# Row sums of the last norm carried through the additions in memory, and three of its tiles shared out to ScalarE and GpSimd

## The chip, the core and the metric

The kernel runs on one core of a Trainium2 chip. The metric is the device time of one execution in microseconds. The core's engines are TensorE (PE; its weight loads are PEld), VectorE (DVE), ScalarE (ACT), GpSimd (POOL) and SyncE (SP), which only issues transfers here. On-chip memory is SBUF (128 partitions) and PSUM (8 banks of 512 float32 columns in each partition), into which TensorE writes.

## The reference

One layer of a hybrid decoder for 1024 prompt rows and 8 sample rows of width 1024. A mixer of four branches comes first, then a first norm, a mixture of 16 SwiGLU experts of which each row uses two, and a last norm:

```
x <- LN(ALPHA * x + Mixer(x));  x <- LN(ALPHA * x + MoE(x))

def layer_norm(x, g, b):
    xf = x.astype(jnp.float32)
    mu = xf.mean(-1, keepdims=True)
    var = jnp.square(xf - mu).mean(-1, keepdims=True)
    return ((xf - mu) * lax.rsqrt(var + LN_EPS) * g + b).astype(x.dtype)

    out = jnp.zeros(xt.shape, jnp.float32)
    for e in range(N_EXPERTS):
        h = jax.nn.silu(xt @ w1_l[e]) * (xt @ w3_l[e])
        out = out + gate[:, e:e + 1] * (h @ w2_l[e])
```

## The kernel before, in words

The 1032 rows are nine tiles of 128 (the sample tile, number 0 in the order used here, has 8 rows). Every large product is made of three products of parts: an operand is split into a rounded part and its remainder, ScalarE making the first (`w13_high`, `w2_high`, `rows_high`), VectorE the second (`w13_low`, `w2_low`, `rows_low`).

After the mixer each tile gets its first norm (`normed`, the row x1 in `acc`), the router picks two experts for each row, and the rows are scattered by GpSimd's indirect transfers into a buffer in memory ordered by expert (`xs`, rows of `DX` columns: the 1024 of x1, then two gate columns, the group's top expert and the row's number). SP also writes x1 itself to a buffer in memory, `yd` (`store_x1`).

Then 32 work items follow, each up to 128 rows of one expert (16 experts, 16 possible overflows). In item q TensorE makes the hidden product of item q+1 in two halves (`hidden`), transposes the rows of item q+2, then the down product of item q (`down`) in two halves of 512 columns. ScalarE takes each half out of PSUM, times the row's gate, into one of four buffers `yo` (`out_low`, L1002 and L1004), and GpSimd adds the buffer into the rows of `yd` by an accumulating indirect transfer (`add_rows`, L1593). Items that can share rows wait for each other's additions. `yd` thus ends as x1 plus the experts' sum (divided by ALPHA, which the norm takes out).

The end: SP loads the last norm's weights `ln2` (L567, L568), waits for all additions, loads the nine tiles of `yd` back into `acc` (L574) and stores each finished tile (L579). For each tile ScalarE makes a pass for the row sum (L1054), scales it to minus the mean (L1056), makes a pass for the sum of squares (L1058) and a square root (L1060); VectorE's `finish` takes the reciprocal (L1565) and makes two products over the tile (L1567: plus minus-mean, times the weight; L1568: times the reciprocal, plus the bias). The tiles go in the order 0 to 8 on every engine, each engine working through its own list, with semaphores between them (`yg` a tile is loaded, `sd` its square root is there, `y_ready` it is finished). In listings of the program a semaphore that has been used up earlier goes on under its old name.

Of the kernel before, what the change touches and what calls it, by code (L numbers as in the profile page):

```python
# [69 lines left out]
def rows(t):  # L70
    return P if t < NT else NB


def build(nc, a):

    ctx = ExitStack()
    with ctx:
# [3 lines left out]
        def at(off, shape, dt=F32):  # L81
            names[0] += 1
            return ctx.enter_context(placed(nc, f"b{names[0]}_{off}", shape, dt, BASE + off))
# [14 lines left out]
            "sums_T": ("qk_tr_qkc", 8), "sums_nat": ("lsuf", 1), "high": ("qkT_qkc", 8), "y_sample": ("qk_tr_qka", 8),  # L98
# [216 lines left out]
        DX = D + 4  # L315
# [54 lines left out]
        assert 8192 + 8 * DX + 16384 <= TOKB  # L370
# [44 lines left out]
        fs = at(o, [P, 4, 8]); o += 128  # L415
# [26 lines left out]
        def emit_sp2(sp):  # L442
# [128 lines left out]
            for s in range(NT + 1):  # L571
                t = WORDER[s]
                r = rows(t)
                sp.dma_start(acc[0:r, s, 0:D], a["yd"][t * P:t * P + r, :]).then_inc(S(f"yg{s}"), 16)  # L574
            for s in range(NT + 1):
                t = WORDER[s]
                sp.wait_ge(S("y_ready"), s + 1)
                dst = a["y_p"][t * P:(t + 1) * P, :] if t < NT else a["y_s"]
                sp.dma_start(dst, acc[0:rows(t), s, 0:D]).then_inc(S("out"), 16)  # L579
# [285 lines left out]
        def emit_act2(act):  # L865
# [128 lines left out]
            def out_low(q):  # L994
                u = q % 2
                act.wait_ge(S("dna"), N("dna", q + 1))
                act.wait_ge(S("xl"), N("xl", 2 * (q + 1)))
                if q >= 4:
                    act.wait_ge(S(f"ys{q % 4}"), N(f"ys{q % 4}", 16 * (q // 4)))
                elif q == 2:  # L1000
                    rows_left()
                act.activation(yo[q % 4][:, 0:512], ps[:, 2, :], ACT.Copy, scale=gt[:, q % 4, 1:2]).then_inc(S("ya"), 1)  # L1002
                act.wait_ge(S("down"), N("down", q + 1))
                act.activation(yo[q % 4][:, 512:D], ps[:, 3, :], ACT.Copy, scale=gt[:, q % 4, 1:2]).then_inc(S("yb"), 1)  # L1004
# [41 lines left out]

            for s in range(NT + 1):
                r = rows(WORDER[s])
                z = acc[0:r, s, 0:D]
                f = fs[0:r, s % 4]  # L1050
                if s >= 4:
                    act.wait_ge(S("y_ready"), s - 3)
                act.wait_ge(S(f"yg{s}"), 16)
                act.activation(junk[0:r, :], z, ACT.Identity, accum_out=f[:, 0:1]).then_inc(S("sums"), 1)  # L1054
                act.wait_ge(S("sums"), 3 * s + 1)
                act.activation(f[:, 1:2], f[:, 0:1], ACT.Copy, scale=-1.0 / D).then_inc(S("sums"), 1)  # L1056
                act.wait_ge(S("sums"), 3 * s + 2)
                act.activation(junk[0:r, :], z, ACT.Square, bias=f[:, 1:2], accum_out=f[:, 2:3]).then_inc(S("sums"), 1)  # L1058
                act.wait_ge(S("sums"), 3 * s + 3)
                act.activation(f[:, 3:4], f[:, 2:3], ACT.Sqrt, scale=1.0 / D, bias=epsb[0:r, :]).then_inc(S("sd"), 1)  # L1060

        def emit_dve2(dve, link, out_high, last_item):
# [237 lines left out]
            dve.tensor_copy(acc[:, :, D + 3], rt["token"][:])  # L1300
# [109 lines left out]
            def place(b):  # L1410
# [80 lines left out]
            def rows_low(q):  # L1491
# [5 lines left out]
                dve.tensor_scalar(rt["to"][:, q % 8:q % 8 + 1], xg[:, u, D + 3:D + 4], 0.0 if e < NE else rt["unused"][:, e - NE:e - NE + 1],  # L1497
                                  4096.0, ALU.add, ALU.add)
                link(dve.tensor_scalar(mine[:, 0:1], xg[:, u, D + 2:D + 3], first, None, ALU.is_equal))
                dve.scalar_tensor_tensor(mine[:, 1:2], xg[:, u, D:D + 1], mine[:, 0:1], xg[:, u, D + 1:D + 2], ALU.mult, ALU.add)  # L1500
# [72 lines left out]
        def emit_pool2(pool):  # L1573
# [1088 lines left out]
def split_k(w):  # L2662
# [11 lines left out]
SCRATCH = {"f_dram": ((H, SEQ), F32), "s_dram": ((NB, SW), F32), "self_dram": ((2, NB * H), F32), "tb_dram": ((H, P * TBW), F32), "xs": ((SLOTS, D + 4), F32),  # L2674
           "yd": ((TOK, D), F32)}
# [42 lines left out]
```

## Time and profile before

| | us |
|---|---|
| median of 3 runs | 1358.37 (1356.71 to 1361.46) |
| the profiled execution | 1356.65 |
| its span, first to last instruction | 1354.8 |
| TensorE busy | 1277.8 (94%) |
| VectorE busy | 939.8 (69%) |
| ScalarE busy | 615.4 (45%) |
| GpSimd busy | 226.6 (17%) |

The shares are means over stages with different limits. The line of 40 slices shows TensorE at nine tenths until the last two slices of 34 us each, where it falls to 7 and to 0 while VectorE and ScalarE stay busy. Times in the rows below count from the span's start.

### The profile page before, as it was taken

How to read it: one execution, taken by the hardware profiler on the slowest of the kernel's cores; microseconds unless marked ns; L12 is line 12 of the kernel's file. 1: busy time of each engine (PE TensorE's matmuls, PEld its weight loads, DVE VectorE, ACT ScalarE, POOL GpSimd, SP SyncE). 2: the span in 40 equal slices, each digit the busy share in tenths (PEclk: the TensorE clock that was granted, in tenths of full speed). 3: DMA queues.
4: the chain of work that ended last, by engine and by line, in shares of the span. 5: the costliest groups of instructions: out<-in, count | busy, mean ns of one | idle time of the engine just before them, and what ended most of it. 6: DMA issues, size and time to landing. Idle time of an engine off the chain costs nothing.

```text
span 1354.8 us, 20040 instructions
## 1 busy us (share of the span) xinstructions
PE 1277.8 (94%) x7652; PEld 1079.2 (80%) x7652; DVE 939.8 (69%) x1490; ACT 615.4 (45%) x918; POOL 226.6 (17%) x199
## 2 busy tenths in 40 slices
PE   8999999998999999999999999999999999999970
PEld 5788657785579999999999999878657788888850
DVE  3574455424557888989888434576788899999957
ACT  4452565422752212232211121222338789888867
POOL 0200000007022232212110000000366221211130
PEclk9999999999999999999999999989899999999995
DMA  8123301002036767556653522322699986778986
GB/s 251 36 107 114 138 1 35 25 5 94 1 115 217 245 231 262 175 157 225 214 168 122 193 72 90 131 89 70 227 348 380 352 271 226 283 246 308 404 215 250
DMA packets 75012, 240.23 MB, mean 177 GB/s; under 512 B 16661, under 2 KB 27140, under 8 KB 61086
## 3 DMA queue, kind: packets, MB, share of 16 engines
q1 hardware_dynamic: 48630, 160.80, 33.0%
q0 software_dynamic: 17584, 61.31, 14.7%
q10 hardware_dynamic: 8704, 16.84, 3.7%
q8 instruction: 61, 1.00, 0.3%
q14 instruction: 33, 0.27, 0.1%
HBM read 215.65 MB, written 65.76 MB: 208 GB/s over the span
## 4 chain that ended last, share of the span: by engine, by line
PE 77%; DVE 5%; ACT 4%; DMA 3%; issue 3%; POOL 2%; POOLq 0%; ACTq 0%; DVEq 0%; SPq 0%
PE ps L592 18%; PE ps L594 17%; PE ps L593 17%; PE ps L1720 5%; PE ps L1751 3%; PE ps L1752 3%; PE ps L1753 3%; PE ps L1883 3%; PE ps L1923 2%; POOL tmp_xs L1577 2%; DMA b<-in_w 1%; DMA tmp_xs<-b,b 1%; ACT b L1058 1%; ACT b L1054 1%; PE ps L1915 1%
## 5 line engine op out<-in xcount | busy, mean ns | idle before, releaser
L592 PE MATMUL ps<-b,b 128*128 128x344 f32 (+1 forms) x1472 | 518.0, 352 | 4.5 <-DVE b L1530 2.6
L594 PE MATMUL ps<-b,b 128*128 128x344 f32 (+1 forms) x1472 | 509.0, 346 | 0.0
L593 PE MATMUL ps<-b,b 128*128 128x344 f32 (+1 forms) x1472 | 508.6, 345 | 0.0
L592 PEld LDWEIGHTS ps<-b,b 128*128 128x128 f32 x1472 | 277.5, 188 | 30.2 <-issue 8.2
L594 PEld LDWEIGHTS ps<-b,b 128*128 128x128 f32 x1472 | 277.1, 188 | 22.2
L593 PEld LDWEIGHTS ps<-b,b 128*128 128x128 f32 x1472 | 277.4, 188 | 18.7
L905 ACT ACTIVATE b<-ps,b 128x344 f32<-128x344 f32 x96 | 52.7, 549 | 312.7 <-PE ps L594 312.7
L1489 DVE TENSOR_TENSOR b<-b,b 128x2048 fp32r<-128x2048 f32 x64 | 146.6, 2292 | 15.7 <-ACT b L970 14.3
L1720 PE MATMUL ps<-b,b 128*128 128x128 f32 (+1 forms) x794 | 115.9, 277 | 16.4 <-DVE b L1352 3.0
L970 ACT CAST b<-b 128x2048 fp32r<-128x2048 f32 x64 | 123.6, 1933 | 6.2 <-DMA b<-in_w 4.0
L1720 PEld LDWEIGHTS ps<-b,b 128*128 128x128 f32 (+1 forms) x794 | 91.8, 143 | 43.4 <-issue 5.9
L1751 PE MATMUL ps<-b,b 128*128 128x512 f32 (+1 forms) x312 | 119.2, 382 | 1.5 <-DVE b L2207 1.4
L1752 PE MATMUL ps<-b,b 128*128 128x512 f32 (+1 forms) x312 | 116.6, 374 | 0.0
L1753 PE MATMUL ps<-b,b 128*128 128x512 f32 (+1 forms) x312 | 116.1, 372 | 0.0
L1266 DVE TENSOR_TENSOR b<-b,ps 128x344 f32<-128x344 f32 x72 | 36.8, 511 | 95.0 <-PE ps L594 85.8
L1593 POOL DMA_INDIRECT tmp_yd<-b,b x32 | 65.4, 2044 | 215.7 <-DMA tmp_yd<-b,b 118.8
L2207 DVE TENSOR_TENSOR b<-b,b 128x1024 fp32r<-128x1024 f32 x40 | 48.9, 1224 | 67.8 <-ACT b L2056 66.8
L1577 POOL DMA_INDIRECT tmp_xs<-b,b x36 | 49.8, 1384 | 275.1 <-issue 256.5
L2368 DVE CUSTOM_DVE_ANT_0 b<-ps,b 128x128 f32<-128x128 f32 (+7 forms) x64 | 45.9, 756 | 42.8 <-PE ps L1883 21.9
L1525 DVE TENSOR_TENSOR b<-b,b 128x2048 fp32r<-128x2048 f32 x32 | 73.1, 2285 | 1.4 <-ACT b L1012 1.4
L1751 PEld LDWEIGHTS ps<-b,b 128*128 128x128 f32 x312 | 59.3, 190 | 13.9 <-issue 3.3
L2056 ACT CAST b<-b 128x1024 fp32r<-128x1024 f32 x40 | 42.0, 1049 | 61.9 <-PE ps L1753 55.8
(308 smaller groups left out, 1610.1 us busy)
## 6 DMA issues: line engine op xcount, KB each, us to landing
b<-in_w SPq DMA_DIRECT2D x96, 1024.0 KB
b<-in_w_merge SPq DMA_DIRECT2D x32, 640.5 KB, 5.1
tmp_xs<-b ACTq DMA_DIRECT2D x32, 514.0 KB, 6.0
b<-tmp_xs SPq DMA_DIRECT2D x32, 514.0 KB
b<-in_w_in SPq DMA_DIRECT2D x6, 1024.0 KB, 7.4
b<-in_xT SPq DMA_DIRECT2D x4, 1024.0 KB, 12.4
b<-in_w_out SPq DMA_DIRECT2D x4, 1024.0 KB, 7.2
b<-in_x SPq DMA_DIRECT2D x8, 512.0 KB, 4.1
```

Source lines behind the costliest of these rows:

```text
L592: mm(out, hi, mhi, start=start, stop=False)
L593: mm(out, hi, mlo, start=False, stop=False)
L594: return mm(out, lo, mhi, start=False, stop=stop)
L970: act.copy(w13_hi[w13_slot(m)][:].rearrange("p k n -> p (k n)"), w13_raw[m % 4][:].rearrange("p k n -> p (k n)")).then_inc(S("w13h"), 1)
L1489: dve.tensor_tensor(lo, raw, hi.bitcast(F32), ALU.subtract).then_inc(S("w13l"), 1)
L1525: dve.tensor_tensor(lo, raw, hi.bitcast(F32), ALU.subtract).then_inc(S("w2l"), 1)
L1577: pool.indirect_dma_start(a["xs"], bass.IndirectOffsetOnAxis(rt[slots][0:r, s, c:c + 1], 0), acc[0:r, s, :], None, bounds_check=bound, oob ...
L1593: pool.indirect_dma_start(a["yd"], bass.IndirectOffsetOnAxis(rt["to"][:, q % 8:q % 8 + 1], 0), yo[q % 4][:], None, bounds_check=TOK - 1, o ...
L1720: return nc.tensor.transpose(out, in_, ident[0:n, 0:n])
L1751: mm(ps[:, j % 2, 0:cw], hi, whi, start=(k == 0), stop=False)
L1752: mm(ps[:, j % 2, 0:cw], hi, wlo, start=False, stop=False)
L1753: m = mm(ps[:, j % 2, 0:cw], lo, whi, start=False, stop=(k == KD - 1))
```

## The change

The width of `yd`, of `yo` and of the first part of `acc` becomes `DY` = D + 2 = 1026. The first norm's last product writes the row sum of x1 into column D (column D+1 is set to zero once), and each of the two evictions in `out_low` writes the row sum of its half into a column of its own, so that the additions in memory also add up the row sums. At the end ScalarE scales and sums these two columns, which gives minus the mean, and makes only the pass for the squares. ScalarE first copies `ln2` into four banks of PSUM, from where VectorE reads it. For tiles 1, 3 and 6 (`BY_POOL`) VectorE makes the first product only; ScalarE multiplies by the reciprocal, behind its work for the next tile, and GpSimd adds the bias. SP stores in the order of `STORED`. Buffers are moved for the wider rows.

```
+        BY_POOL = (1, 3, 6)
+        STORED = (0, 2, 1, 4, 5, 3, 7, 6, 8)
...
-        yo = [at(o, [P, D]) for o in (MT + 8192 + 8 * DX, MT + 12288 + 8 * DX, RING, RING + 4096)]
+        yo = [at(o, [P, DY]) for o in (MT + 8192 + 8 * DX, MT + 12320 + 8 * DX, RING, RING + 32768)]
...
-                act.activation(yo[q % 4][:, 0:512], ps[:, 2, :], ACT.Copy, scale=gt[:, q % 4, 1:2]).then_inc(S("ya"), 1)
+                act.activation(yo[q % 4][:, 0:512], ps[:, 2, :], ACT.Copy, scale=gt[:, q % 4, 1:2], accum_out=yo[q % 4][:, D:D + 1]
+                               ).then_inc(S("ya"), 1)
...
+            act.wait_ge(S("ln2"), 32)
+            act.copy(ps[:, 4:6, :].rearrange("p a b -> p (a b)"), ln2[:, 0, :])
+            act.copy(ps[:, 6:8, :].rearrange("p a b -> p (a b)"), ln2[:, 1, :]).then_inc(S("ln2_ps"), 1)
+
+            def moments_of(s):
+                r = rows(WORDER[s])
+                f = fs[0:r, s]
+                act.wait_ge(S(f"yg{s}"), 16)
+                act.activation(junk[0:r, 0:2], acc[0:r, s, D:DY], ACT.Copy, scale=-1.0 / D, accum_out=f[:, 1:2]).then_inc(S("sums"), 1)
+                act.wait_ge(S("sums"), 2 * s + 1)
+                act.activation(junk[0:r, :], acc[0:r, s, 0:D], ACT.Square, bias=f[:, 1:2], accum_out=f[:, 2:3]).then_inc(S("sums"), 1)
...
+                moments_of(s)
+                if s - 1 in BY_POOL:
+                    z = acc[:, s - 1, 0:D]
+                    act.wait_ge(S("shifted"), N("shifted", BY_POOL.index(s - 1) + 1))
+                    act.activation(z, z, ACT.Copy, scale=fs[:, s - 1, 4:5]).then_inc(S("scaled"), 1)
...
-                dve.scalar_tensor_tensor(z, z, rv[0:r, 0:1], ln1[1][0:r, :], ALU.mult, ALU.add).then_inc(S("x1"), 1)
+                dve.scalar_tensor_tensor(z, z, rv[0:r, 0:1], ln1[1][0:r, :], ALU.mult, ALU.add, accum_out=acc[0:r, s, D:D + 1]
+                                         ).then_inc(S("x1"), 1)
...
+                dve.wait_ge(S("ln2_ps"), N("ln2_ps", 1))
+                if s in BY_POOL:
+                    dve.scalar_tensor_tensor(z, z, f[:, 1:2], g, ALU.add, ALU.mult).then_inc(S("shifted"), 1)
+                    return
+                link(dve.scalar_tensor_tensor(z, z, f[:, 1:2], g, ALU.add, ALU.mult))
+                dve.scalar_tensor_tensor(z, z, f[:, 4:5], b, ALU.mult, ALU.add).then_inc(S("y_ready"), 1)
...
+            pool.wait_ge(S("ln2"), 32)
+            for n, s in enumerate(BY_POOL):
+                z = acc[:, s, 0:D]
+                pool.wait_ge(S("scaled"), N("scaled", n + 1))
+                pool.tensor_tensor(z, z, ln2[:, 1, :], ALU.add).then_inc(S("y_pool"), 1)
```

ScalarE's list before, tiles 0 and 1 of the last norm (`b_99072` is `acc`, `b_33024` scratch, `b_138368` the statistics):

```order
L1054 ACTIVATE b_33024_221,b_138368_262<-b_99072_184 8x1024 [waits yg0]
L1056 ACTIVATE b_138368_262<-b_138368_262 8x1 [waits sums]
L1058 ACTIVATE b_33024_221,b_138368_262<-b_99072_184,b_138368_262 8x1024 [waits sums]
L1060 ACTIVATE b_138368_262<-b_138368_262,b_138336_261 8x1 [waits sums]
L1054 ACTIVATE b_33024_221,b_138368_262<-b_99072_184 128x1024 [waits yg1]
```

ScalarE's list in the changed program from the copies of `ln2` (`b_168960`), then tiles 0 to 2 and the copy for tile 1 (`band_mm` goes on as `shifted`):

```order
L1057 COPY ps<-b_168960_220 128x1024 [waits ln2]
L1058 COPY ps<-b_168960_220 128x1024
L1064 ACTIVATE b_33024_221,b_138432_262<-b_99072_184 8x2 [waits yg0]
L1066 ACTIVATE b_33024_221,b_138432_262<-b_99072_184,b_138432_262 8x1024 [waits sums]
L1068 ACTIVATE b_138432_262<-b_138432_262,b_138400_261 8x1 [waits sums]
L1064 ACTIVATE b_33024_221,b_138432_262<-b_99072_184 128x2 [waits yg1]
L1066 ACTIVATE b_33024_221,b_138432_262<-b_99072_184,b_138432_262 128x1024 [waits sums]
L1068 ACTIVATE b_138432_262<-b_138432_262,b_138400_261 128x1 [waits sums]
L1064 ACTIVATE b_33024_221,b_138432_262<-b_99072_184 128x2 [waits yg2]
L1066 ACTIVATE b_33024_221,b_138432_262<-b_99072_184,b_138432_262 128x1024 [waits sums]
L1068 ACTIVATE b_138432_262<-b_138432_262,b_138400_261 128x1 [waits sums]
L1075 ACTIVATE b_99072_184<-b_99072_184,b_138432_262 128x1024 [waits band_mm]
```

A tile has three instructions for four, the first over 2 columns for 1024, and the copy for tile 1 stands behind tile 2.

VectorE's list before, tiles 0 and 1:

```order
L1565 RECIPROCAL b_138368_262<-b_138368_262 8x1 [waits sd]
L1567 SCALAR_TENSOR_TENSOR b_99072_184<-b_99072_184,b_138368_262,b_168960_220 8x1024 [waits ln2,dve_chain]
L1568 SCALAR_TENSOR_TENSOR b_99072_184<-b_99072_184,b_138368_262,b_168960_220 8x1024 [waits dve_chain]
L1565 RECIPROCAL b_138368_262<-b_138368_262 128x1 [waits sd]
L1567 SCALAR_TENSOR_TENSOR b_99072_184<-b_99072_184,b_138368_262,b_168960_220 128x1024 [waits ln2,dve_chain]
```

VectorE's list in the changed program, tiles 0 and 1 and the start of 2 (`d_tr` goes on as `ln2_ps`):

```order
L1583 RECIPROCAL b_138432_262<-b_138432_262 8x1 [waits sd]
L1588 SCALAR_TENSOR_TENSOR b_99072_184<-b_99072_184,b_138432_262,ps 8x1024 [waits d_tr,dve_chain]
L1589 SCALAR_TENSOR_TENSOR b_99072_184<-b_99072_184,b_138432_262,ps 8x1024 [waits dve_chain]
L1583 RECIPROCAL b_138432_262<-b_138432_262 128x1 [waits sd]
L1586 SCALAR_TENSOR_TENSOR b_99072_184<-b_99072_184,b_138432_262,ps 128x1024 [waits d_tr,dve_chain]
L1583 RECIPROCAL b_138432_262<-b_138432_262 128x1 [waits sd]
L1588 SCALAR_TENSOR_TENSOR b_99072_184<-b_99072_184,b_138432_262,ps 128x1024 [waits d_tr,dve_chain]
```

The second input is PSUM for SBUF, and tile 1 has one product for two.

## Rows read from the trace of the kernel before

**Rows 1.** Windows: length; busy PE, PEld, DVE, ACT, POOL; clock; DMA share; GB/s.

```profile
1200.00:1250.00 50.00, 50.00 (x248) 41.35 (x247) 48.25 (x54) 43.47 (x50) 8.84 (x6) 1.00 0.84 297
...
1322.80:1352.00 29.20, 0.00 (x0) 0.00 (x0) 24.56 (x27) 25.22 (x54) 0.00 (x0) 0.50 0.67 267
```

**Rows 2.** The chain that ended last, from 1312: start, us, what.

```profile
1312.80 0.70 ACT b L1004
...
1314.47 6.29 DMA tmp_yd<-b,b
1320.84 1.94 DMA b<-tmp_yd
...
1350.49 1.28 DVE b L1568
```

**Rows 3.** Timeline of ScalarE, tile 2 of the last norm: start, us, what.

```profile
1328.56 1.04 ACT L1054 ACTIVATE b<-b 128x1024 f32<-128x1024 f32 x1
1329.51 0.18 ACT L1054 ACTIVATION_READ_ACCUMULATOR b<-b 128x1 f32 x1
1329.73 0.20 ACT L1056 ACTIVATE b<-b 128x1 f32<-128x1 f32 x1
1329.96 1.15 ACT L1058 ACTIVATE b<-b,b 128x1024 f32<-128x1024 f32 x1
...
1331.24 0.29 ACT L1060 ACTIVATE b<-b,b 128x1 f32<-128x1 f32 x1
1331.44 1.04 ACT L1054 ACTIVATE b<-b 128x1024 f32<-128x1024 f32 x1
```

**Rows 4.** Timeline of VectorE, the same tile.

```profile
1331.56 0.16 DVE L1565 RECIPROCAL b<-b 128x1 f32<-128x1 f32 x1
1331.76 1.28 DVE L1567 SCALAR_TENSOR_TENSOR b<-b,b,b 128x1024 f32<-128x1024 f32 x1
1333.08 1.28 DVE L1568 SCALAR_TENSOR_TENSOR b<-b,b,b 128x1024 f32<-128x1024 f32 x1
```

**Rows 5.** Groups by line and shape: busy us, mean ns, idle before.

```profile
L2537 POOL TENSOR_TENSOR b<-b,b 128x1032 fp32r<-128x1032 f32 x8 | 19.0, 2372 | 0.6
...
L1319 DVE SCALAR_TENSOR_TENSOR b<-b,ps 128x512 f32<-128x512 f32 x16 | 10.4, 684 | 22.5 <-PE ps L594 22.2 <-DVE b L1429 0.2
...
L2270 DVE SCALAR_TENSOR_TENSOR b<-ps,b,b 128x512 f32<-128x512 f32 x4 | 3.0, 751 | 3.9 <-PE ps L1806 3.7
...
L2368 DVE DVE_READ_ACCUMULATOR2_ANT b<- 128x1 f32 x64 | 5.3, 83 | 0.0
```

**Rows 6.** Timelines of GpSimd and VectorE around 340.

```profile
339.38 2.38 POOL L2537 TENSOR_TENSOR b<-b,b 128x1032 fp32r<-128x1032 f32 x1
...
340.55 0.69 DVE L2368 CUSTOM_DVE_ANT_0 b<-ps,b 128x512 f32<-128x512 f32 x1 [0.51 <-PE ps L1883]
```

**Rows 7.** The load L574 issued between 1321.1 and 1321.6 (tile 1).

```profile
DMA to landing us min/median/max: 3.6/3.6/3.6
```

**Rows 8.** Timeline of VectorE, ScalarE and TensorE in one item, around 1298.

```profile
1294.46 2.29 DVE L1489 TENSOR_TENSOR b<-b,b 128x2048 fp32r<-128x2048 f32 x1 [0.21 <-ACT b L970]
...
1295.40 0.39 ACT L986 ACTIVATE b<-ps 128x256 f32<-128x256 f32 x1 [0.97 <-PE ps L594]
...
1298.81 2.29 DVE L1489 TENSOR_TENSOR b<-b,b 128x2048 fp32r<-128x2048 f32 x1
...
1298.98 0.48 PE L592 MATMUL ps<-b,b 128*128 128x512 f32 x1
...
1301.84 0.40 PE L592 MATMUL ps<-b,b 128*128 128x512 f32 x1
```

**Rows 9.** The chain of waits between 1060 and 1090.

```profile
1062.97 13.91 DMA b<-in_w
```

**Rows 10.** Queues: packets, MB, share of 16 engines; 956:966, then 1320:1356.

```profile
q0 software_dynamic: 569, 1.95, 51.0%
...
q1 hardware_dynamic: 2336, 8.46, 59.9%
```

More of the change, by code:

```diff
@@ L573, in emit_sp2 @@
                 r = rows(t)
-                sp.dma_start(acc[0:r, s, 0:D], a["yd"][t * P:t * P + r, :]).then_inc(S(f"yg{s}"), 16)
-            for s in range(NT + 1):
+                sp.dma_start(acc[0:r, s, 0:DY], a["yd"][t * P:t * P + r, :]).then_inc(S(f"yg{s}"), 16)
+            for s in STORED:
                 t = WORDER[s]
-                sp.wait_ge(S("y_ready"), s + 1)
+                if s in BY_POOL:
+                    sp.wait_ge(S("y_pool"), N("y_pool", BY_POOL.index(s) + 1))
+                else:
+                    sp.wait_ge(S("y_ready"), sum(x <= s and x not in BY_POOL for x in range(NT + 1)))
                 dst = a["y_p"][t * P:(t + 1) * P, :] if t < NT else a["y_s"]
@@ L1045, in emit_act2 @@
                     act.activation(fs[:, 0, 6:7], epsb[:], ACT.Sqrt)
-            for s in range(NT + 1):
[L1048 to L1060, printed above, removed]
+            act.wait_ge(S("ln2"), 32)
[8 more added lines that the diff above has]
+                act.activation(junk[0:r, :], acc[0:r, s, 0:D], ACT.Square, bias=f[:, 1:2], accum_out=f[:, 2:3]).then_inc(S("sums"), 1)
+                act.wait_ge(S("sums"), 2 * s + 2)
+                act.activation(f[:, 3:4], f[:, 2:3], ACT.Sqrt, scale=1.0 / D, bias=epsb[0:r, :]).then_inc(S("sd"), 1)
+            for s in range(NT + 1):
+                moments_of(s)
[3 more added lines that the diff above has]
+                    act.activation(z, z, ACT.Copy, scale=fs[:, s - 1, 4:5]).then_inc(S("scaled"), 1)
         def emit_dve2(dve, link, out_high, last_item):
@@ L1496, in rows_low @@
                 first = float(NE - e) if e < NE else rt["first_e"][:, e - NE:e - NE + 1]
[L1497 removed]
+                dve.tensor_scalar(rt["to"][:, q % 8:q % 8 + 1], xg[:, u, DY + 3:DY + 4], 0.0 if e < NE else rt["unused"][:, e - NE:e - NE + 1],
                                   4096.0, ALU.add, ALU.add)
[L1499 to L1500 removed]
+                link(dve.tensor_scalar(mine[:, 0:1], xg[:, u, DY + 2:DY + 3], first, None, ALU.is_equal))
+                dve.scalar_tensor_tensor(mine[:, 1:2], xg[:, u, DY:DY + 1], mine[:, 0:1], xg[:, u, DY + 1:DY + 2], ALU.mult, ALU.add)
                 for half in range(2):
@@ L1562, in finish @@
                 z = acc[0:r, s, 0:D]
-                f = fs[0:r, s % 4]
+                f = fs[0:r, s]
+                g, b = (ps[0:r, k:k + 2, :].rearrange("p a b -> p (a b)") for k in (4, 6))
                 dve.wait_ge(S("sd"), NT + 1 + s + 2)
                 link(dve.reciprocal(f[:, 4:5], f[:, 3:4]))
-                dve.wait_ge(S("ln2"), 32)
-                link(dve.scalar_tensor_tensor(z, z, f[:, 1:2], ln2[0:r, 0, :], ALU.add, ALU.mult))
-                dve.scalar_tensor_tensor(z, z, f[:, 4:5], ln2[0:r, 1, :], ALU.mult, ALU.add).then_inc(S("y_ready"), 1)
+                dve.wait_ge(S("ln2_ps"), N("ln2_ps", 1))
+                if s in BY_POOL:
+                    dve.scalar_tensor_tensor(z, z, f[:, 1:2], g, ALU.add, ALU.mult).then_inc(S("shifted"), 1)
+                    return
+                link(dve.scalar_tensor_tensor(z, z, f[:, 1:2], g, ALU.add, ALU.mult))
+                dve.scalar_tensor_tensor(z, z, f[:, 4:5], b, ALU.mult, ALU.add).then_inc(S("y_ready"), 1)
             for s in range(NT + 1):
```

31 lines of the change are left out of this document (17 added, 14 removed).

## The prediction

> **What bounds the kernel now.** I read the windows first, then the chain of waits over the end, then the timelines of ScalarE, VectorE and GpSimd there, and last the experts, since the change puts instructions there too. The windows [rows 1] show two regimes. In the experts' stage TensorE is busy 50.00 of 50 us; VectorE (48.25) and ScalarE (43.47) lie beneath it, VectorE with little room. From 1322.8 to 1352 us TensorE does nothing, and ScalarE (25.22) and VectorE (24.56 of 29.2) alternate: this is the last norm. So the gain can only come from the end, and a loss can come from anywhere.
>
> The chain [rows 2] gives the end in order: ScalarE's last eviction at 1312.80, the last addition into memory at 1314.47 (6.29 us), the load of the first tile at 1320.84 (1.94 us), after which ScalarE's first sum starts at 1322.80, and VectorE's last multiply at 1350.49. It ends at 1351.77; 3.03 us more to the end of the span of 1354.8 are the last store.
>
> A tile costs ScalarE 2.88 us (1328.56 to 1331.44) [rows 3]: the row sum takes from 1328.56 to 1329.73, its scaling 0.23, the squares 1.28 (to 1331.24), the square root 0.20. VectorE [rows 4] needs 0.20 for the reciprocal, 1.32 for the first product, 1.28 for the second, 2.80 together, and its reciprocal starts 0.32 after ScalarE's square root starts. Both engines thus need 2.8 to 2.9 us for each of nine tiles, ScalarE slightly more. My sum of the end by these durations gives 1351.8 where the trace has 1351.77.
>
> **The change, the end.** ScalarE loses the pass over 1024 columns. In its place stands one instruction over two columns, which scales and sums at once: 0.20 (the scaling of one column [rows 3]) and about 0.12 for its accumulator read, of which 0.10 overlaps: 0.32. A tile then costs 0.32 + 1.28 + 0.20 = 1.80 us. The bounds are 0.23 (no read at all) and 1.18 (as the full pass); 0.32 is worked out from the nearest row of that size. Three tiles (1, 3, 6) add one scaled copy over 1024 columns, 1.06 each by the start of the squares' accumulator read, which is the same shape with a pointer operand.
>
> VectorE does both products for six tiles (2.80 + 0.02) and one for three (1.52). Its second tensor is now in PSUM. No row has this product at 1024 columns, so I bound it: with both inputs in SBUF it takes 1.28 [rows 4]; at 512 columns with a PSUM input 0.684 and 0.751 [rows 5]. Another 512 columns cost at most 1.28 - 0.684 = 0.60, which gives 1.28 to 1.35. I take 1.28; the far end is 1.50, twice the 0.751.
>
> Stepping through both engines: the first sum starts at 1322.80 + 0.22 = 1323.02, since the last eviction now ends with an accumulator read (start to next start 0.22 1329.51 to 1329.73 [rows 3]). Tile 1 lands 3.6 us after its issue near 1321.4 [rows 7], so at about 1325.0, when ScalarE asks for it; later ones come faster than ScalarE's 1.80. VectorE's reciprocals then start at 1324.9, 1327.8, 1329.3, 1332.3, 1334.1, 1337.0, 1339.8, 1341.3 and 1344.3. The three copies on ScalarE start at 1329.3, 1334.0 and 1341.4; the first and third wait 0.7 and 0.9 us for VectorE's product, and what is queued behind them is ScalarE's work for tiles 3 and 8, for which VectorE then waits 0.5 and 0.2 us. VectorE ends at 1347.14.
>
> GpSimd's addition over 1032 columns takes 2.37 us [rows 5], so 2.35 here. Behind the copies it ends at 1332.8, 1337.5 and 1344.9. The stores are issued in the order 0, 2, 1, 4, 5, 3, 7, 6, 8 on SP; tile 6 is ready 2.3 us before tile 8, so no late GpSimd tile holds the last one, and the last store keeps its 3.03 us. The two copies of the norm's weights into PSUM (about 1 us each) lie in ScalarE's wait between 1313.5 and 1322.8 and would cost nothing until the load came 7 us sooner. The end thus gains 1351.77 - 1347.14 = 4.6 us.
>
> One row speaks for GpSimd and VectorE running side by side: GpSimd's addition at 339.38 lasts 2.38 us, and VectorE's instruction over 512 columns of PSUM and SBUF, wholly beside it at 340.55, lasts 0.69 [rows 6], like the 0.684 of the product alone [rows 5]. The Trainium skill (SBUF — State Buffer, SBUF: two separate sides) says that a VectorE instruction with two SBUF inputs and a GpSimd one that reads SBUF exclude each other for their whole length; by that rule alone the product with `ln2` in SBUF would lose up to 2.35 us per GpSimd tile, and the one with a PSUM input nothing. The trace agrees for PSUM; no run here yet shows the SBUF case.
>
> **The change, the experts.** Each of 32 experts' evictions gets two accumulator reads, 0.44 us on ScalarE. Followed through one period [rows 8]: ScalarE idles 0.97 before its activation at 1295.40, which TensorE gates, so 0.44 does not add up from expert to expert. It does delay the weight copy (L970) ahead of that wait, for whose end VectorE's subtraction at 1294.46 waits (0.21 idle), and what follows it. The nearest limit is the subtraction at 1298.81: it ends at 1301.10, and TensorE needs its result for the second half of the hidden product at 1301.84 (the first of its products starts at 1298.98). 0.74 of room against at most 0.44: nothing is lost. Below nothing is excluded, as no instruction leaves this stage.
>
> In one place ScalarE and VectorE are themselves the chain: in the first experts, after the last scattered rows have landed, it runs from ScalarE's evictions through VectorE's subtractions to a weight load at 1062.97 of 13.91 us [rows 9]. The 0.44 stands in that path once; the load behind it is limited by traffic and may take it in. I charge 0.35, with 0 and 0.9 as ends. The row sum of x1 gives nine VectorE products an accumulator read of 0.083 [rows 5]; one is on the path (the last tile's), 0.1. Together 0.45.
>
> **Memory.** Rows grow from 4096 to 4104 bytes, 0.2%. The rows of 4112 bytes that are scattered already move at 1.95 MB in 51.0% of 10 us of 16 engines, 23.9 GB/s for each; those of 4096 at 8.46 MB in 59.9% of 36 us, 24.5 [rows 10]: up to 2.5% for the odd length. On 6.29 us that is under 0.2, on the loads nothing, as they are not waited for after tile 1. I charge 0 and keep 0.2 in the range. Against the change speaks the Trainium skill (DMA: Bandwidth & Descriptors, How a descriptor splits into AXI transactions): a transfer that starts off a 256-byte boundary reads from the boundary below, which makes of a 4104-byte row 17 pieces for 16, an estimate of 6% or up to 0.4 us on the last addition. The rows of 4112 bytes start off such boundaries too and show less.
>
> **Sum.** 4.63 - 0.45 = 4.2 us. The profiled execution took 1356.65, of which 1354.8 are span; it becomes 1352.5. The median of the three runs shown is 1.7 above it, so on the median the forecast is 1358.37 - 4.2 = 1354.2.
>
> **Rivals.**
> *A, the reads set the experts' pace (slower).* Point of decision: VectorE's subtraction at 1298.81 ends over 0.74 us later. For: VectorE's subtraction at 1294.46 waits for ScalarE's copy [rows 8], and VectorE is idle for only 1.75 of 50 us [rows 1]. Against: ScalarE is gated by TensorE each period and gives the 0.44 back. If it isn't given back, 30 periods cost 0.44 each, 13.2 us: 1354.2 + 13.2 = 1367.4.
> *B, a row of 4104 bytes becomes two packets.* For: no accumulating transfer with such rows is in the trace. Against: 569 packets carry 1.95 MB, so 4112 bytes go as one. Eight rows per engine and tile at 0.148 us a packet (345 engine-us over 2336 packets) add 1.2 us to the last addition and 1.2 us to each load; the loads then land every 2.6 us, the ninth near 1345, and VectorE ends near 1350.4: gain 1.0, 1357.4.
> *C, GpSimd's additions shut VectorE out.* Against: rows 6. It would be decided by one VectorE product stretched to over 2 us beside an addition; each of three additions shifts VectorE by 2.35, and the sum of the end then comes to 1353.45: 1.7 later than before, with the 0.45 2.1: 1360.5.
> *D, the products are slower from PSUM* (1.50 for 1.28): VectorE ends at 1349.8, gain 1.5, 1356.9.
>
> **How the numbers follow.** Forecast 0.61, its own range 1352.4 to 1356.2; A 0.07, B 0.12, C 0.06, D 0.08, a larger loss in the stages before the experts 0.06. Three tenths of a per cent, 4.1 us, is about what a measurement of this kernel can tell from no change, and my gain stands right at it: of the forecast's 0.61 about 0.45 lies beyond and 0.16 within, as the 0.45 us charged in the experts may also be nothing. B, C and D lie within (0.26), A and the loss in earlier stages beyond on the slow side. Faster 0.45, same 0.42, slower 0.13. The range leaves out A: 1351.0 to 1359.5.
>
> **What would show it.** Right: the first sum of two columns takes about 0.3 us from start to start, ScalarE's period 1.8; VectorE's last product ends 4 to 5 us nearer to the last addition's landing than before; GpSimd's additions last 2.35 us; TensorE's gaps in the experts stay as they were. Wrong: TensorE with gaps in front of the hidden product's second half (A), the last addition over 7 us or loads landing over 2 us apart (B), a VectorE product over 2 us (C) or near 1.5 (D), or the third copy on ScalarE waiting over 1 us.

## The result: slower, by half a per cent

The changed kernel takes 1365.77 us (median of 17 runs, 1361.83 to 1370.46) where the kernel before took 1359.02 beside it: ratio 1.0053, 95% interval 1.004 to 1.0066. Measured again later (e13_again) it was 1.0026 (1.0013 to 1.0039). Two of the twelve executions of e13_again, at mean granted clocks of 0.56 and 0.65, took 2120 and 1827 us; its ratio leaves them out, its median of 1363.56 us does not. The forecast of 1354.2 and its range of 1351.0 to 1359.5 were wrong, and so was the sign. The profiled execution took 1364.58, its span is 1362.8, 8.0 more than before.

The last norm itself did what was forecast. ScalarE's last eviction with the copy behind it, from its timeline, and then the chain that ended last (start, us, what):

```profile
1321.00 0.69 ACT L1012 ACTIVATE b<-ps,b 128x512 f32<-128x512 f32 x1 [0.61 <-PE ps L601]
1321.68 1.01 ACT L1057 COPY ps<-b 128x1024 f32<-128x1024 f32 x1
```

```profile
1322.76 8.18 DMA tmp_yd<-b,b
1331.40 3.97 DMA b<-tmp_yd
...
1355.32 1.28 DVE b L1589
```

The loads are issued at 1331.02, 8.26 us after the last addition (SyncE's first load; [rows 2] had 6.37 by the same reckoning). From there VectorE needs 25.58 us to its end at 1356.60, for 30.93 from 1320.84 to 1351.77: 5.35 us gained. One tile on ScalarE, and its scaled copy:

```profile
1341.89 0.19 ACT L1064 ACTIVATE b<-b 128x2 f32<-128x2 f32 x1
1341.98 0.19 ACT L1064 ACTIVATION_READ_ACCUMULATOR b<-b 128x1 f32 x1
1342.20 1.15 ACT L1066 ACTIVATE b<-b,b 128x1024 f32<-128x1024 f32 x1
...
1343.47 0.29 ACT L1068 ACTIVATE b<-b,b 128x1 f32<-128x1 f32 x1
1343.67 1.13 ACT L1075 ACTIVATE b<-b,b 128x1024 f32<-128x1024 f32 x1
1344.71 0.19 ACT L1064 ACTIVATE b<-b 128x2 f32<-128x2 f32 x1
```

The sum of two columns takes 0.31 from start to start where [rows 3] had 1.17 for the pass over 1024 and 0.23 for its scaling. By line and shape (busy, mean ns), VectorE's products from PSUM keep the 1.28 us of [rows 4], and GpSimd's additions take 2.1:

```profile
L1588 DVE SCALAR_TENSOR_TENSOR b<-b,b,ps 128x1024 f32<-128x1024 f32 x5 | 6.4, 1281 | 0.2
L1628 POOL TENSOR_TENSOR b<-b,b 128x1024 f32<-128x1024 f32 x3 | 6.4, 2118 | 23.8 <-ACT b L1075 23.8
```

The experts' windows answer [rows 1]: TensorE is full, ScalarE has 44.84 us for 43.47.

```profile
1200.00:1250.00 50.00, 50.00 (x249) 41.43 (x248) 48.03 (x56) 44.84 (x59) 12.51 (x6) 1.00 0.87 282
```

The time was lost in three other places. The first lies between 950 and 1010 us, where x1's rows are scattered. The chain there:

```profile
990.20 0.97 POOL tmp_xs L1598
991.48 14.76 DMA tmp_xs<-b,b
1006.31 3.76 DMA b<-tmp_xs
1010.11 1.13 PE ps L1746 x4
```

SyncE could load the first expert's rows at 1006.31; in the kernel before, the same load was issued at 997.78:

```profile
997.78 0.81 SPq L514 DMA_DIRECT2D b<-tmp_xs  x2
```

The rows are asked for 8.5 us later, and the last eviction starts at 1321.00 for 1312.80: 8.2 us later. TensorE's wait for the rows, after and before, grew by more than that:

```profile
PE ps L1746 <- DMA b<-tmp_xs: 12.1, 1, 12.1
```

```profile
PE ps L1720 <- DMA b<-tmp_xs: 0.5, 1, 0.5
```

The 0.5 belongs to that one execution, in which TensorE came to the wait about 3 us later than after the change (its last block of work ahead of it starts at 989.47, for 986.61). In e4_reads, which has the rows of before, TensorE waits 3.1 us. The queues from 985 to 996 (packets, MB, share of 16 engines), first before, then after:

```profile
DMA packets 1412, 4.15 MB, mean 378 GB/s; under 512 B 402, under 2 KB 402, under 8 KB 1411
...
q0 software_dynamic: 1084, 3.00, 68.7%
q1 hardware_dynamic: 327, 1.14, 25.7%
```

```profile
DMA packets 736, 2.66 MB, mean 242 GB/s; under 512 B 90, under 2 KB 90, under 8 KB 735
...
q0 software_dynamic: 397, 1.46, 63.2%
q1 hardware_dynamic: 338, 1.19, 48.9%
```

q0 carries the scatters, q1 the stores of x1. Nearly the same share of the engines' time moved half the scattered bytes. Share times 16 engines times 11 us, over the MB, is what one MB costs: 40 us of an engine before and 76 after for the scatters, 40 and 72 for the stores. There were not more packets for the same bytes: from 956 to 966, with the scatters alone, there were 579 in 1.99 MB where [rows 10] had 569 in 1.95. Even there one MB cost 44.9 for 41.8:

```profile
q0 software_dynamic: 579, 1.99, 55.8%
```

The second place is the last addition (1.9 us). Slower packets explain little of it: from its issue to its landing one MB costs 108 us of an engine, 102 before. But 0.78 MB moved in that time, for 0.54 before, and one addition is 0.53 MB. The addition ahead of it took 10.2 us (6.1 before) and was still under way for 5 us (0.8 before):

```profile
1317.61 1.55 POOL L1614 DMA_INDIRECT tmp_yd<-b,b  x1 [3.65 <-ACT b L1012]
```

What slowed the additions ahead of the last one is not shown. The third is behind VectorE's last product: 6.2 us to the end of the span for 3.03 before. GpSimd's last addition stands here:

```profile
1352.07 2.36 POOL L1628 TENSOR_TENSOR b<-b,b 128x1024 f32<-128x1024 f32 x1 [5.19 <-ACT b L1075]
```

8.2 + 0.1 (before the addition's issue) + 1.9 - 5.35 + 3.2 = 8.0, the difference of the spans.

### The profile page after: what moved, and what is told of

It reads as the page before. It is cut to its first block, busy times and chain, and to the rows that moved or that the text cites. A ratio compares the mean times of both kernels' runs of the same rounds, so it can differ in the third digit from the quotient of the medians.

```text
span 1362.8 us, 20106 instructions
## 1 busy us (share of the span) xinstructions
PE 1276.7 (94%) x7652; PEld 1079.6 (79%) x7652; DVE 934.9 (69%) x1497; ACT 617.4 (45%) x978; POOL 221.6 (16%) x202
## 4 chain that ended last, share of the span: by engine, by line
PE 77%; DMA 5%; DVE 4%; ACT 4%; issue 2%; POOL 0%; SPq 0%; ACTq 0%; DVEq 0%; POOLq 0%
PE ps L599 18%; PE ps L601 18%; PE ps L600 18%; PE ps L1746 5%; PE ps L1777 3%; PE ps L1778 3%; PE ps L1779 3%; PE ps L1909 3%; PE ps L1949 2%; DMA tmp_yd<-b,b 2%; DMA b<-in_w 1%; DMA tmp_xs<-b,b 1%; PE ps L1941 1%; ACT b L977 1%; ACT b L1066 1%
## 5 line engine op out<-in xcount | busy, mean ns | idle before, releaser
L1614 POOL DMA_INDIRECT tmp_yd<-b,b x32 | 61.6, 1924 | 237.5 <-DMA tmp_yd<-b,b 135.0
L1598 POOL DMA_INDIRECT tmp_xs<-b,b x36 | 42.3, 1175 | 273.2 <-issue 256.5
```

Of the source, the lines that this page charges most:

```text
L1614: pool.indirect_dma_start(a["yd"], bass.IndirectOffsetOnAxis(rt["to"][:, q % 8:q % 8 + 1], 0), yo[q % 4][:], None, bounds_check=TOK - 1, o ...
```

## Experiments

Each was timed beside the kernel before. A ratio compares runs that stood beside each other, so it is not the quotient of two medians. Where e1_rows16 is the base, its own edit is included. The column "scatter" is the time, in one profiled execution, from the issue of the scatter that releases the first expert's rows to its landing. The column "per MB" is the engine time that one MB of the scatters cost from 985 to 996, worked out as above from the same execution.

| kernel | row bytes yd, xs | ratio to before (95%) | scatter us | per MB us |
|---|---|---|---|---|
| kernel before | 4096, 4112 | 1 | 4.0 | 40 |
| changed kernel | 4104, 4120 | 1.0053 (1.0040 to 1.0066) | 14.76 | 76 |
| e13_again | 4104, 4120 | 1.0026 (1.0013 to 1.0039) | 12.53 | 56 |
| e17_gap | 4104, 4120 | 1.0018 (1.0004 to 1.0031) | 10.88 | 52 |
| e3_yd4104 | 4104, 4112 | 1.0024 (1.0010 to 1.0037) | 9.56 | 55 |
| e15_xs4128 | 4104, 4128 | 0.9988 (0.9975 to 1.0002) | 8.28 | 53 |
| e2_xs4120 | 4096, 4120 | 1.0009 (0.9997 to 1.0021) | 7.60 | 47 |
| e4_reads | 4096, 4112 | 0.9997 (0.9985 to 1.0009) | 5.95 | 41 |
| e11_sbuf4120 | 4096, 4112 | 0.9996 (0.9984 to 1.0008) | 5.95 | 40 |
| e12_yd4100 | 4100, 4112 | 1.0000 (0.9985 to 1.0015) | 6.65 | 41 |
| e14_rows4 | 4108, 4124 | 0.9982 (0.9966 to 0.9998) | 6.30 | 41 |
| e16_xs4136 | 4112, 4136 | 0.9984 (0.9971 to 0.9996) | 6.57 | 41 |
| e1_rows16 | 4112, 4128 | 0.9979 (0.9965 to 0.9994) | 6.65 | 41 |
| e18_gap16 | 4112, 4128 | 0.9976 (0.9965 to 0.9988) | 6.59 | 41 |
| e7_rows32 | 4128, 4160 | 0.9983 (0.9971 to 0.9996) | 6.18 | 41 |

The kernel before issued that scatter later in its profiled execution (993.66, for 989.90 in e4_reads), so its 4.0 us is no measure of a faster transfer; the cost per MB doesn't depend on the issue. In e13_again and e17_gap the scatters come some 3 us later, and from 996 to 1006 one MB costs 71 and 66. The two lengths can be told apart. With the scatters alone, from 956 to 966, one MB costs 44.0 to 44.9 in the four kernels with xs rows of 4120 bytes and 40.1 to 42.3 in all others of the table: 4120 alone makes the scatters some 7% dearer. With the stores of x1 beside them, yd rows of 4104 bytes make them some 30% dearer (53 and 55 for 41), and both lengths together up to 76.

### Rows or reads: e1_rows16, e2_xs4120, e3_yd4104, e4_reads

**e1_rows16**, the changed kernel with two columns more in each row:

```diff
-        DY = D + 2
+        DY = D + 4
...
+                if q < 4:
+                    act.activation(yo[q][:, D + 2:DY], epsb[:].to_broadcast([P, 2]), ACT.Copy, scale=0.0)
...
-                act.activation(junk[0:r, 0:2], acc[0:r, s, D:DY], ACT.Copy, scale=-1.0 / D, accum_out=f[:, 1:2]).then_inc(S("sums"), 1)
+                act.activation(junk[0:r, 0:2], acc[0:r, s, D:D + 2], ACT.Copy, scale=-1.0 / D, accum_out=f[:, 1:2]).then_inc(S("sums"), 1)
```

> The changed kernel with two unused columns more per row: rows of yd have 4112 bytes (16 x 257), rows of xs 4128 (16 x 258), so every row in memory starts on a multiple of 16 bytes again; in the changed kernel they had 4104 and 4120, only multiples of 8. Theory 1 (rows that start on a multiple of 8 bytes alone slow the scatters, the stores and the additions): the 8.2 us before the experts and the 1.9 us of the last addition come back, the gain of the end of 5.3 us stays; 1353 to 1356 us where the kernel before takes 1359; the last addition about 6.4 us, median scatter landing from 985 to 996 us near 6 us instead of 15. Theory 2 (the accumulator reads of the experts and of x1 cost the 8.2 us): nothing changes, 1365 to 1366. Theory 3 (longer rows as such, whatever their start): still slower than the changed kernel, 1366 or more.

1356.88 us, 0.9979. The chain has the scatter at 6.65 us and the last addition at 6.12:

```profile
990.94 6.65 DMA tmp_xs<-b,b
...
1318.11 6.12 DMA tmp_yd<-b,b
```

Theory 1 holds in its size, theories 2 and 3 fall. By its median it is a microsecond above the expected range; the profiled execution shows one piece. The last expert's last product ran with the clock granted at 0.63 on average, mostly at its lower level of 1.2 GHz, and took 4.6 us where before it took 3.1 at 2.4 GHz (stretch, length, TensorE busy, clock, DMA share, GB/s; first e1_rows16, then before):

```profile
1311.70:1316.30 4.60, 4.59 (x12) 0.63 1.00 248
```

```profile
1309.70:1312.80 3.10, 3.04 (x12) 1.00 1.00 267
```

In front of it TensorE had nothing to do for 2.0 and 1.9 us. The profiled executions of e2_xs4120 and e3_yd4104 show such a stretch at the lower clock too, those of the changed kernel and e4_reads don't: it comes and goes, and a single profile must be corrected for it.

**e2_xs4120**, the kernel before with longer rows of xs (`DX = D + 6`, and `dve.memset(acc[:, :, D + 4:DX], 0.0)` ahead of the router's columns):

> The kernel before with rows of xs of 4120 bytes instead of 4112 (two columns of zeros behind the four of the router), everything else as before. Theory 1, scattered rows to blame: 6 to 8 us slower, 1365 to 1367, with late scatters and TensorE's wait for tmp_xs near 12 us; the last addition stays at 6.4 us. Theory 1, rows of yd to blame: within 1 us of 1359. Theory 2 (accumulator reads): 1359.

1360.56 us, 1.0009. Less than expected, and by the time alone not clear of no change (0.9997 to 1.0021); the scatter shows it:

```profile
989.53 7.60 DMA tmp_xs<-b,b
```

**e3_yd4104**, the kernel before with `yo` tiles and rows of yd of 4104 bytes, the two columns zero:

```diff
-                sp.dma_start(a["yd"][t * P:t * P + r, :], acc[0:r, s, 0:D]).then_inc(S("xd"), 16)
+                sp.dma_start(a["yd"][t * P:t * P + r, 0:D], acc[0:r, s, 0:D]).then_inc(S("xd"), 16)
...
-           "yd": ((TOK, D), F32)}
+           "yd": ((TOK, D + 2), F32)}
```

> The kernel before with rows of yd 4104 bytes apart: the additions move 4104 bytes (1024 values and two zeros), the stores of x1 and the loads of the last norm 4096 bytes of each row. Theory 1, rows of yd to blame: last addition 8.3 us for 6.4, and if the stores of x1 collide with the scatters, 5 to 8 us more before the experts: 1361 (addition alone) to 1368. Theory 1, scattered rows to blame: 1361, the addition alone. Theory 2: 1359.

1361.62 us, 1.0024. The scatter writes xs, whose rows are as before, and is slowed all the same; of the two transfers that run then, only the stores of x1 into yd differ from before. They carry 4096 bytes a row as before, 4104 apart, so for yd it is the distance between the rows that counts, not what is moved of them. The last addition takes 6.75:

```profile
989.86 9.56 DMA tmp_xs<-b,b
...
1319.86 6.75 DMA tmp_yd<-b,b
```

**e4_reads**, the kernel before with accumulator outputs on both evictions and x1's last product, into spare columns (`accum_out=sm[...]`):

> The kernel before with the accumulator reads alone: both evictions of each expert and x1's last product get an accumulator output (into 16 spare columns of SBUF); no row in memory grows and the last norm is as before. Theory 2 (the reads cost the time before the experts): 1365 to 1367, with TensorE waiting 12 us for tmp_xs. Theory 1: 1359 to 1359.5, as the reads lie in ScalarE's idle time and one VectorE read of 0.1 us is on the path.

1357.90 us for 1357.85, 0.9997: the reads cost nothing.

```profile
989.90 5.95 DMA tmp_xs<-b,b
```

So the longer rows cost what was lost before the experts, and the accumulator reads nothing that this can tell. One kind of row alone cost 1.2 us (within the noise) and 3.3 us by the ratios; both together, in the changed kernel, more.

### The end of the program: e5_pool13, e6_nopool, e7_rows32, e8_pool134

In the traces of the changed kernel and of e1_rows16 the span ends 8.3 us after GpSimd's last addition (1354.43 to 1362.8, 1347.70 to 1356.0), and no packet moves in the last 3.8 to 4 us of it. Before, GpSimd had issued its last addition at 1316. That was the new theory G, with the stores as its rival.

**e5_pool13**: e1_rows16 with `BY_POOL = (1, 3)` and `STORED = (0, 2, 1, 4, 3, 5, 6, 7, 8)`.

> The kernel of e1_rows16 (rows on multiples of 16 bytes) with two tiles for GpSimd (1 and 3) instead of three (1, 3 and 6). Theory G (GpSimd needs 8.3 us from its last addition to the end of the program: 1347.70 to 1356.0 in e1_rows16, 1354.43 to 1362.8 in the changed kernel): GpSimd's last addition now ends 17.4 us after the issue of the first load instead of 23.4, its 8.3 us are covered, and the program ends 3.0 to 3.1 us after VectorE, whose end is 0.6 us later by the stepping (26.2 us after the load for 25.6): 29.3 us for 31.7, so 2.4 us faster than e1_rows16, about 1354.5. Rival S (the stores of tiles 7, 6 and 8 fall together and delay the end): their last packets ran until 1352 of 1356.0 in e1_rows16, so little can be won there; VectorE's later end counts and it takes 1357.5.

1353.24 us, 0.9967. By the time alone its gain over three tiles is not clear of noise (e7_rows32, measured beside it with the norm of e1_rows16: 0.9983, the intervals overlap); the trace decides for G. GpSimd ends at 1335.60, VectorE at 1345.90, the span 3.1 us later:

```profile
core 0 of [0], span 1349.0 us
...
1344.62 1.28 DVE L1591 SCALAR_TENSOR_TENSOR b<-b,b,ps 128x1024 f32<-128x1024 f32 x1
```

**e6_nopool**: e1_rows16 with `BY_POOL = ()` and the stores in the order 0 to 8.

> The kernel of e1_rows16 with no tile for GpSimd: VectorE finishes all nine, ScalarE makes no scaled copy; the two sums carried through the additions stay, and the second tensor stays in PSUM. VectorE then sets the end: 2.2 + 9 x 2.82 = 27.6 to 28.8 us after the issue of the first load. Theory G: 3.0 us more to the end, 30.6 to 31.8 us for e1_rows16's 31.7: 1356 to 1357, no slower than with three tiles on GpSimd. Rival S or an end that costs 6.1 us whatever GpSimd does: 33.7 to 34.9, 1359 to 1360.

1357.70 us, 0.9984, as three tiles on GpSimd. VectorE ends at 1349.77, 28.3 us after the load's issue, and the span 3.1 after it:

```profile
core 0 of [0], span 1352.9 us
...
1348.49 1.28 DVE L1591 SCALAR_TENSOR_TENSOR b<-b,b,ps 128x1024 f32<-128x1024 f32 x1
```

**e7_rows32**: e1_rows16 with `DY = D + 8`, `DX = D + 16`.

> The kernel of e1_rows16 with rows of yd of 4128 bytes (32 x 129) and of xs of 4160 (32 x 130) instead of 4112 (16 x 257) and 4128: multiples of 32. If a start on a multiple of 16 is all that matters: as e1_rows16, 1356.9 within 0.7, scatter that releases the first rows about 6.6 us, last addition 6.1. If each doubling brings more: the first rows land 1 us sooner, the last addition under 6 us, 1355 to 1356. If the length counts: 1357.5 to 1358.

1356.91 us, 0.9983: no more than multiples of 16 give.

**e8_pool134**: e1_rows16 with other tiles for GpSimd, and ScalarE's copy one tile later:

```diff
-        BY_POOL = (1, 3, 6)
-        STORED = (0, 2, 1, 4, 5, 3, 7, 6, 8)
+        BY_POOL = (1, 3, 4)
+        STORED = (0, 2, 1, 5, 3, 6, 4, 7, 8)
...
-                if s - 1 in BY_POOL:
-                    z = acc[:, s - 1, 0:D]
+                if s - 2 in BY_POOL:
+                    z = acc[:, s - 2, 0:D]
```

> The kernel of e1_rows16 with tiles 1, 3 and 4 for GpSimd and ScalarE's scaled copy of a tile put behind the moments of the second tile after it instead of the first. Theory G: GpSimd's last addition ends 20.1 us after the issue of the first load, so its 8.3 us end with the last store; ScalarE no longer waits for VectorE's product before a copy (0.68 us for the third in e1_rows16), VectorE ends after 25.1 us; 28.2 to 28.5 us to the end for 31.7: 3.2 us faster than e1_rows16, 1353.7, and faster than both kernels. Rival S: 1356.4.

1350.22 us (7 runs), ratio 0.9945 (0.9925 to 0.9966), faster than both kernels and clear of e7_rows32 beside it. GpSimd ends at 1338.79, and 1338.79 + 8.3 = 1347.1 is the end of the span; VectorE had ended at 1343.68:

```profile
core 0 of [0], span 1347.1 us
...
1336.43 2.36 POOL L1630 TENSOR_TENSOR b<-b,b 128x1024 f32<-128x1024 f32 x1 [0.47 <-ACT b L1077]
```

### GpSimd's end by itself, and two more row lengths: e9_late_op to e12_yd4100

**e9_late_op**, the kernel before with this at GpSimd's end:

```diff
+            pool.wait_ge(S("y_ready"), NT + 1)
+            pool.memset(rt["s"][:, 0, :], 0.0)
```

> The kernel before with one more instruction: GpSimd waits for VectorE's last product and then writes zeros to 16 columns nobody reads. Theory G (the program ends 8.3 us after GpSimd's last work): VectorE's end (3.0 us before the end of the span) plus 0.2 to 0.4 for the write plus 8.3: 5.5 to 5.7 us slower, 1364 for 1358.6. Rival (GpSimd's end is not what the program waits for): 1358.6.

1363.72 us, 1.0044 (1.0028 to 1.0059), 5.1 us more. The write takes 0.11 us; 8.3 us later the span ends:

```profile
core 0 of [0], span 1362.0 us
...
1353.60 0.11 POOL L1604 MEMSET b<- 128x16 f32 x1 [35.78 <-DVE b L1568]
```

**e10_late_wait**, only the first of these lines:

> As e9_late_op without the write: GpSimd only waits for VectorE's last product. If the 8.3 us begin when GpSimd has passed its last instruction of any kind, it is again 5.3 us slower, 1364. If only work on its vector lanes starts them: 1358.6.

1362.84 us, 1.0038 (1.0019 to 1.0056). VectorE's last product ends at 1352.35 and the span at 1360.9, 8.55 later:

```profile
core 0 of [0], span 1360.9 us
...
1351.07 1.28 DVE L1568 SCALAR_TENSOR_TENSOR b<-b,b,b 128x1024 f32<-128x1024 f32 x1
```

So a late wait on GpSimd is enough, whether it works or not. Theory G is shown: the end of the span waits for GpSimd's end plus 8.3 us. What fills the 8.3 us no run shows.

**e11_sbuf4120**, the kernel before with the tile of x1 at `D + 6` columns in SBUF alone:

> The kernel before with the tile of x1 at 4120 bytes a row in SBUF instead of 4112, so that each tile's first byte there moves to a multiple of 8; all rows in memory keep 4096 and 4112 bytes. Theory 1 (rows in memory): no change, 1358.6 within 1. If the start in SBUF is to blame: as e2_xs4120, 1 to 2 us slower with scatters of 7.6 us where e4_reads has 5.95.

1357.67 us, 0.9996, scatter 5.95: at this length the start in SBUF doesn't matter, the rows in memory do.

**e12_yd4100**, e3_yd4104 with one column for two (`DY = D + 1`):

> As e3_yd4104 with rows of yd 4100 bytes apart (4 x 1025), so most rows start on a multiple of 4 or 8 alone. If a start off a multiple of 16 is what costs (three rows of four here, one of two in e3_yd4104): more than e3_yd4104's 3.3 us, 4 to 6 us slower than before: 1363 to 1364.5. If it is the length beyond 4096: less than or as e3_yd4104, 1361 to 1362.

1358.00 us, 1.0000, scatter 6.65. This was not expected: such rows start on multiples of 16 even less often than those of 4104, and cost nothing. Theory 1 as I had put it, a start off a multiple of 16, fell.

### What it is about the rows: e13_again to e18_gap16

**e13_again**, the changed kernel again:

> The changed kernel itself once more (rows of yd 4104 bytes, of xs 4120), beside the next three on the same chip. If its loss is a matter of the program: 1.0053 of before within the interval of then (1.004 to 1.0066). If it belongs to the chip of the first measurement: nearer to e1_rows16's 0.998.

1363.56 us, 1.0026; scatter and last addition are late again (12.53 and 7.72):

```profile
994.33 12.53 DMA tmp_xs<-b,b
...
1325.78 7.72 DMA tmp_yd<-b,b
```

**e14_rows4**, the changed kernel with `DY = D + 3`, `DX = D + 7` (an odd number of columns, so the transfers that clear xs beforehand are split unevenly):

> The changed kernel with rows of yd of 4108 bytes (4 x 1027) and of xs of 4124 (4 x 1031). Theory 8 (rows that are odd multiples of 8 bytes are slow, odd multiples of 4 are not): as e1_rows16, 0.998 of before, scatter that releases the first rows 6 to 7 us. Theory 16 (all rows that are not multiples of 16 are slow, and e12_yd4100 did not show it because its x1 rows were stored with 4096 bytes): 1.005 or more, scatter 15 us.

1356.86 us, 0.9982, as good as rows that are multiples of 16 bytes:

```profile
991.58 6.30 DMA tmp_xs<-b,b
```

**e15_xs4128**, the changed kernel with xs at `D + 8` columns, yd as changed:

> The changed kernel with rows of xs of 4128 bytes (multiple of 16) and of yd of 4104 as changed. If rows of yd are the larger cause (e3_yd4104 alone cost 0.0024 of the time, e2_xs4120 0.0009): 1.002 to 1.003 of before, scatter 9 to 10 us, last addition 7 to 8.3. If both together are needed for the 15 us: 1.000.

1357.83 us, 0.9988: better than expected. The scatter is still slow, the last addition (6.21) no longer:

```profile
992.49 8.28 DMA tmp_xs<-b,b
...
1319.44 6.21 DMA tmp_yd<-b,b
```

**e16_xs4136**, yd at `D + 4`, xs at `D + 10`:

> The changed kernel with rows of yd of 4112 bytes (multiple of 16) and of xs of 4136 (8 x 517). Theory 8 and theory 16 alike: the additions are whole again (6.2 us), the scatters a little slow (7.6 us as in e2_xs4120): 0.999 of before. If the scattered rows were the larger cause: 1.003 or more.

1356.38 us, 0.9984, scatter 6.57. An odd multiple of 8 bytes in xs (8 x 517) costs nothing here, while 8 x 515 in e2_xs4120 cost 1.65 us of scatter.

**e17_gap**, the changed kernel with `"gap": ((8192,), F32)` between xs and yd in memory:

> The changed kernel with 32 KB that nobody uses between xs and yd in memory: rows stay 4104 and 4120 bytes, yd starts where it starts in e1_rows16. Length theory: as the changed kernel, 1.003 to 1.005 of before, first scatter 12 to 15 us, last addition 7.7 to 8.3 us. Place theory: 0.999 to 1.000, scatter under 9, last addition 6.2.

1360.15 us, 1.0018. The scatter is slow as the length would have it, the last addition is back at 6.2 us:

```profile
994.24 10.88 DMA tmp_xs<-b,b
...
1324.53 6.20 DMA tmp_yd<-b,b
```

**e18_gap16**, e1_rows16 with a gap of 480 KB, which puts yd exactly 512 KB farther from the start of xs than in the changed kernel:

> The kernel of e1_rows16 (rows 4112 and 4128 bytes) with 480 KB that nobody uses between xs and yd, so that yd starts on a multiple of 512 KB as in the changed kernel. Length theory: as e1_rows16, 0.998 of before, scatter 6.1 to 6.7 us, last addition 6.2. Place theory: 1.003 or more with scatters of 12 us.

1355.06 us, 0.9976, scatter 6.59: the place of yd within 512 KB that it has in the changed kernel costs nothing alone. The row lengths decide the scatter. The last addition was slow (over 7 us) only in the two executions in which both lengths and the start of yd were those of the changed kernel; that is consistent with a part for the place, but rests on single profiles, and in both the addition before it was still under way.

## Why the prediction was wrong

**The step that failed first: Memory, "I charge 0 and keep 0.2 in the range".** In the profiled execution the loss was 8.2 us before the experts and 1.9 on the last addition, 10.1 together. On one chip, over all its runs, e13_again against e14_rows4 and e16_xs4136 gives 1.0026 - 0.9983 = 0.0043, 5.8 us, for the row lengths alone. Two errors lay in the step. From rows of 4096 and 4112 bytes [rows 10] I concluded that an odd length costs 2.5% at most, but the two measured lengths say nothing of a third: 4104 and 4120 are slow, and among those tried no others are. And I priced the longer row only where I looked for it, at the additions and loads of the end. Stores of such rows run beside the scatters from 973 us on, and [rows 10] already had the engines half busy with the scatters alone. The first expert waits for these scatters; a slower packet there is waited for in full.

The Trainium skill (DMA: Bandwidth & Descriptors, How a descriptor splits into AXI transactions) makes a descriptor that does not start on a 256-byte boundary dearer, by the bytes that are fetched from the boundary below and not used. The runs don't agree with it as an explanation: most rows of 4100, 4108, 4112 and 4128 bytes start off such boundaries as well and the scatter stayed at 6.1 to 6.7 us.

**The second: "the last store keeps its 3.03 us".** It became 6.2. I had checked that no tile of GpSimd was stored late, but not what the program does after GpSimd's last instruction: 8.3 us, hidden before behind 35 us of norm, and now from 1354.4 to 1362.8. It is 3.2 us here. In the trace of e5_pool13 the end is 3.1 us behind VectorE again, and e9_late_op shows the cost of a late GpSimd with nothing else changed (1.0044).

**The gain of the norm, up to VectorE's end,** was right in its mechanism and low by 0.7: 5.35 for 4.63. The first sum (0.32 forecast, 0.31), the tile (1.80, 1.79), the product from PSUM (1.28, 1.28), the copy (1.06, 1.04) fit, and the third copy waited 0.68 for 0.9, the first not at all for 0.7; tile 1's load came 0.6 us after ScalarE was ready for it, behind the smallest tile. GpSimd took 2.0 to 2.36 where 2.35 was charged.

**The experts**: 0.45 us charged, nothing measurable (e4_reads, 0.9997, 0.9985 to 1.0009; 0.45 us would be 0.0003).

**The rivals.** A falls by the windows and e4_reads. B's sign, a last addition over 7 us, came, but its mechanism falls: with loads of 4104-byte rows the norm's loads and stores are as many packets as in [rows 10]:

```profile
q1 hardware_dynamic: 2336, 8.46, 67.8%
```

Its direction, slower rows, was right, and its price of 3.2 us for the gain was too small because it too looked at the end alone. C falls: VectorE's products beside GpSimd's additions take 1.28. D falls by the same number. The "larger loss in the stages before the experts" is what came, and had 0.06 because no mechanism stood behind it. The range was said to leave out A alone, but C's 1360.5 lay outside it too.

**Where the gain is.** With rows of 4112 and 4128 bytes and GpSimd out of the way early, the kernel takes 0.9945 of before, some 7.5 us less. The norm with GpSimd's tiles put early but the rows left at 4104 and 4120 bytes wasn't tried.

**What stays open**: why rows of 4104 and 4120 bytes are slow and those of 4100, 4108, 4124 and 4136 aren't, and why the changed kernel came to 1.0053 in one measurement and 1.0026 in another. A start on 16, 8 or 4 bytes doesn't sort them, nor does the place of yd alone or the start in SBUF. Also open is how much of the late last addition belongs to the rows.

## What to carry to other kernels

A row length in memory is a change to every transfer that touches the tensor: price it at the place where the transfers are densest and waited for, not only where the new columns are read, and measure lengths near it (8 bytes more made this kernel faster). Before moving work to an engine that used to finish early, ask what the program does after that engine's last instruction; here GpSimd must be done 8.3 us before the end. An "at most 2.5%" read from two lengths bounds those two.

## What the hardware showed that I had not expected

- The span ends 8.3 us after GpSimd's last instruction if that is late: 8.37, 8.30, 8.31, 8.32 and 8.29 us in the changed kernel, e1_rows16, e8_pool134, e7_rows32 and e9_late_op; 8.55 after VectorE's end behind a wait alone. From VectorE's end, with the last store, it is 3.0 to 3.1 where GpSimd is early.
- From 985 to 996 us one MB of the scatters took 40 us of an engine before and 76 after, with rows 0.2% longer. (Time per packet would overstate it, 0.11 and 0.28 us: 402 of 1412 packets were under 512 bytes before and 90 of 736 after.)
- An accumulator read of 0.19 us on ScalarE starts 0.09 after its short activation (1341.89 to 1341.98) and overlaps it. The pair takes 0.31 to the next start, where the scaling of one column without a read took 0.23 [rows 3].
- GpSimd's addition over 128x1024 took 2.00 us twice and 2.36 once in one execution.
- The last product before the norm ran mostly at the lower clock in one execution (e1_rows16, 0.63) and at the higher in another (the kernel before, 1.00), 1.5 us apart, behind 2.0 and 1.9 us without work.
